# A hybrid encoder layer on one core: seven of eight chunks of the second feed-forward product in Strassen's form, with the weight sums and halves made by GpSimd

## What is computed

```python
x = layer_norm(x, ln_in_g, ln_in_b)
z = x @ w_in                                   # 1024 -> 3088 columns, three head groups
mix = concat(gla(z), stick_breaking_attention(z), short_conv(z)) @ w_out
x = layer_norm(ALPHA * x + mix, ln1_g, ln1_b)
ff = square(relu(x @ w_up)) @ w_down           # 1024 -> 4096 -> 1024
y = layer_norm(ALPHA * x + ff, ln2_g, ln2_b)
```

## Time and profile before

| what | value |
|---|---|
| median of 3 runs | 2981.42 us (2979.93 to 2982.21) |
| the profiled execution, own time | 2985.28 us |
| its span | 2983.5 us |
| TensorE busy | 2712.3 us, 91% of the span, 13798 matmuls |
| VectorE, ScalarE, GpSimd busy | 50%, 35%, 6% |
| granted TensorE clock, mean | 0.95 of full |
| DMA, mean over the span | 171 GB/s |

### The profile page before, as it was taken

One profiled execution on the slowest core, in us unless ns is written; L12 is line 12 of the kernel. 1 busy time (PEld: TensorE's weight loads), 2 busy tenths in 40 slices (PEclk: granted clock), 3 DMA queues, 4 the chain that ended last, 5 costly groups with the idle time before them and its releaser, 6 DMA issues. The chain is left out here.

```text
span 2983.5 us, 38620 instructions
## 1 busy us (share of the span) xinstructions
PE 2712.3 (91%) x13798; PEld 2251.9 (75%) x13798; DVE 1492.7 (50%) x2334; ACT 1040.6 (35%) x1812; POOL 178.5 (6%) x169
## 2 busy tenths in 40 slices
PE   6999999956773889999999999999999889999997
PEld 4787878855552678888778888777888767998985
DVE  6454443348774766656566444456444325422224
ACT  2333332323434343434324344424444321232320
POOL 1000000010000100000011000011000001000001
PEclk9999999978785899999999999999999989999998
DMA  5555454421217455756657666656665544555442
GB/s 195 177 179 169 164 171 133 138 96 37 79 48 234 152 169 183 249 184 200 217 167 236 213 212 209 206 183 204 208 227 188 170 157 155 170 171 161 163 156 95
DMA packets 357275, 509.09 MB, mean 171 GB/s; under 512 B 26656, under 2 KB 209024, under 8 KB 357088
## 3 DMA queue, kind: packets, MB, share of 16 engines
q1 hardware_dynamic: 319840, 466.74, 48.2%
q10 hardware_dynamic: 34576, 31.21, 3.1%
q0 software_dynamic: 2672, 8.66, 0.9%
HBM read 412.07 MB, written 94.45 MB: 170 GB/s over the span
## 5 line engine op out<-in xcount | busy, mean ns | idle before, releaser
L1736 DVE SCALAR_TENSOR_TENSOR p_res<-p_res,p_ps_d 128x512 f32<-128x512 f32 (+1 forms) x340 | 232.1, 685 | 470.5 <-PE p_ps_d L113 464.0
L111 PE MATMUL p_ps_u<-p_xh,p_wh 128*128 128x512 f32 (+1 forms) x1280 | 453.6, 354 | 5.3 <-DVE p_xl L1787 5.3
L112 PE MATMUL p_ps_u<-p_xh,p_wl 128*128 128x512 f32 (+1 forms) x1280 | 452.4, 353 | 0.0
L113 PE MATMUL p_ps_u<-p_xl,p_wh 128*128 128x512 f32 (+1 forms) x1280 | 451.9, 353 | 0.0
L111 PE MATMUL p_ps_d<-p_wh,p_hh 128*128 128x512 f32 (+1 forms) x1088 | 433.1, 398 | 16.6 <-DVE p_res L1736 14.6
L112 PE MATMUL p_ps_d<-p_wh,p_hl 128*128 128x512 f32 (+1 forms) x1088 | 429.4, 395 | 0.0
L113 PE MATMUL p_ps_d<-p_wl,p_hh 128*128 128x512 f32 (+1 forms) x1088 | 428.8, 394 | 0.0
L1650 ACT ACTIVATE p_wh<-p_wst 128x1024 fp32r<-128x1024 f32 x288 | 293.9, 1049 | 274.1 <-PE p_ps_d L113 225.7
L1794 DVE TENSOR_TENSOR p_r<-p_r 128x512 f32<-128x512 f32 (+1 forms) x160 | 95.8, 599 | 464.1 <-ACT p_hh L1680 464.0
L1673 ACT ACTIVATE p_r<-p_ps_u 128x512 f32<-128x512 f32 (+1 forms) x160 | 83.8, 524 | 577.4 <-PE p_ps_u L113 577.4
L111 PEld LDWEIGHTS p_ps_u<-p_xh,p_wh 128*128 128x128 f32 x1280 | 241.8, 189 | 35.6 <-DVE p_xl L1787 6.2
(11 more groups left out here) (161 smaller groups left out, 4299.4 us busy)
## 6 DMA issues: line engine op xcount, KB each, us to landing
p_wl<-wlo_scratch SPq DMA_DIRECT2D x216, 512.0 KB, 5.1
p_wst<-in_w_up SPq DMA_DIRECT2D x128, 512.0 KB, 6.0
p_wst<-in_w_down SPq DMA_DIRECT2D x128, 512.0 KB, 4.7
wlo_scratch<-p_wl SPq DMA_DIRECT2D x72, 512.0 KB, 3.6
p_wst<-in_w_in SPq DMA_DIRECT2D x128, 256.0 KB, 3.4
p_kk<-ks_scratch SPq DMA_DIRECT2D x84, 256.0 KB, 6.2
p_vv<-vs_scratch SPq DMA_DIRECT2D x84, 256.0 KB, 4.7
p_wst<-in_w_out SPq DMA_DIRECT2D x32, 512.0 KB, 5.7
```

What stands on the lines that cost most here:

```text
L111: pe.matmul(out, lhs_hi, rhs_hi, start=first, stop=False, skip_group_check=skip)
L112: pe.matmul(out, lhs_lo, rhs_hi, start=False, stop=False, skip_group_check=skip)
L113: return pe.matmul(out, lhs_hi, rhs_lo, start=False, stop=last, skip_group_check=skip)
L1736: dve.scalar_tensor_tensor(out=acc, in0=acc, scalar=scale, in1=ps_d[:c, d % DB, :], op0=ALU.mult, op1=ALU.add).then_inc(d_free, 1)
```

## The change

**The second product.** A chunk's hidden block (512 tokens by 512 hidden columns) is cut in four quarters, the weights too, and for chunks 0 to 6 seven products of sums of quarters (Winograd's variant, `PRODUCTS`) take the place of eight. A step `product` is two token tiles by two hidden tiles by 512 columns: 12 matmuls. Partial results stay in the PSUM banks and each product adds on to them, and every product's bank is added to `res` by VectorE. Chunk 7 (`PLAIN`) stays as it was, in `down` steps. The 64 tokens of the fifth tile have the plain form as well (`rest`).

**The hidden block.** ScalarE writes ReLU and its square as fp32 to `y`; a new step `split` after the fourth `up` makes four sums (VectorE) and the halves of seven blocks (ScalarE highs, VectorE lows). `mix` rows are staged in `y` too, so their loads wait for the low half of `a22` of chunk 7.

**Its weights.** The sums and both halves of all units of `w_down` are made once, in `phase_in`, by GpSimd, and stored to DRAM as pairs (1 MB for a unit, 60 units); the tail loads pairs and nothing of `w_down` is split there. GpSimd's work goes in 16 steps `halve` ("quads", half a chunk each), put into `order` at equal distances by the matmul columns. The units of `w_up` and `w_out` are split in the first group as before, and stored and loaded back as pairs as well.

**Banks and rings.** `ps_u` and `ps_d` become five banks `ps_d`; `wh` and `wl` become `wp` (four pairs); the stages are two rows of `res`. The planner prices a `product` at 2.7, a `rest` at 1.4.

```diff
+NF = 4
+NCH = D_FF // P // NF
+PLAIN = NCH - 1
+PRODUCTS = ((0, "b11", "a11"), (1, "b21", "a12"), (2, "t2", "s2"), (3, "t1", "s1"), (4, "t3", "s3"), (5, "b22", "s4"), (6, "t4", "a22"))
...
+        quads = [(c, i) for c in range(PLAIN + 1) for i in range(2)]
...
+        began = [x for x, st in enumerate(order) if st[0] == "unit"][len(by_chunk[0]) + 1]
+        spread, passed, n_quad = order[:began], 0.0, 0
...
+                while n_quad < len(quads) and passed * (len(quads) + 0.5) >= n_quad:
+                    spread.append(("halve", n_quad))
+                    n_quad += 1
...
+            def make_halves(x, n, unit, block):
+                c, i, _ = x
+                if n >= 2:
+                    pool.wait_ge(p_out[n % 2], 16 * (n // 2))
+                pool.tensor_copy(ppair[:, n % 2, 0, :], block).then_inc(p_hi, 1)
+                pool.wait_ge(p_hi, n + 1)
+                pool.tensor_tensor(ppair[:, n % 2, 1, :], block, ppair[:, n % 2, 0, :].bitcast(F32), ALU.subtract).then_inc(p_lo, 1)
+                pool.wait_ge(p_lo, n + 1)
+                pool.dma_start(wd_dram[8 * c + DOWN_UNITS.index(unit)].rearrange("p e (f n) -> p e f n", f=2)[:, :, i, :],
+                               ppair[:, n % 2, :, :].bitcast(F32)).then_inc(p_out[n % 2], 16)
...
+            def make_down_weights(x):
+                c, i, n = x
+                pool.wait_ge(p_in, 16 * (quad_no[c, i] + 1))
...
+                for k, (unit, block) in enumerate((("b11", b11), ("b12", b12), ("b21", b21), ("b22", b22))):
+                    make_halves(x, n + k, unit, block)
+                if c != PLAIN:
...
+                    pool.tensor_tensor(b22, b22, b12, ALU.subtract).then_inc(p_sum, 1)
...
+                    pool.tensor_tensor(b12, b12, b11, ALU.subtract).then_inc(p_sum, 1)
...
+                    pool.tensor_tensor(b11, b22, b11, ALU.add).then_inc(p_sum, 1)
...
+                    pool.tensor_tensor(b21, b21, b11, ALU.subtract).then_inc(p_sum, 1)
...
+                    for k, (unit, block) in enumerate((("t3", b22), ("t1", b12), ("t2", b11), ("t4", b21))):
+                        make_halves(x, n + 4 + k, unit, block)
...
+                if what == "halve":
...
+                    make_down_weights((c, i, halves_before[x]))
+                    if x + 1 < len(quads):
+                        pool.wait_ge(p_lo, halves_before[x + 1])
+                        load_down_weights(*quads[x + 1])
                 if what == "norm_a":
...
+        def down_products(g, c):
+            steps = []
+            for n, unit, _ in PRODUCTS:
+                steps.append(("product", g, c, n, weights("down", c, unit)))
+                if unit == "b22" and len(gtiles[g]) > 4:
+                    steps.append(("rest", g, c, weights("down", c, "b12")))
+            return steps
...
             for c in range(NCH - 1):
                 ffn += [up(g, c + 1, f) for f in range(2)]
-                ffn += down(g, c, 0) + down(g, c, 1)
-                if c == NCH - 2 and more:
-                    ffn += [("mix_load", g + 1, k) for k in range(4)]
-                ffn += [up(g, c + 1, f) for f in range(2, NF)]
+                ffn += down_products(g, c)
+                ffn += [up(g, c + 1, f) for f in range(2, NF)] + [("split", g, c + 1)]
             if more:
+                ffn += [("mix_load", g + 1, k) for k in range(4)]
                 ffn += out_steps(g + 1)
...
                     elif g:
-                        sp.wait_ge(d_mm, down_end[(g - 1, NCH - 2)])
+                        sp.wait_ge(blk_lo, lows_of(g - 1, PLAIN, "a22"))
...
+                    wait_unit_used(sp, u)
+                    wait_unit_stored(sp, u)
...
+                    sp.dma_start(wp[:, u % WRING, :, :].bitcast(F32), pair).then_inc(w_arrived[u % WRING], 16)
...
+                elif what == "product":
+                    g, c, n, u = at
...
+                    pe.wait_ge(blk_lo, lows_of(g, c, block))
+                    wait_halves(pe, u)
...
+                    for x in range(2):
+                        b = bank_of[(st, x)]
+                        if bank_free[(st, x)]:
+                            pe.wait_ge(*bank_free[(st, x)])
+                        for i in range(2):
+                            high, low = (t[:, place_of(block), i, P * x:P * x + P] for t in (sh, sl))
+                            mm = split_product(pe, ps_d[:, b, :], high, low, wp[:, u % WRING, 0, 512 * i:512 * i + 512], wp[:, u % WRING, 1, 512 * i:512 * i + 512],
+                                               i == 0 and n in (0, 1, 3), i == 1, skip=True)
+                        mm.then_inc(d_mm, 1)
```

More of the change, by code:

```diff
@@ L234, in phase_in @@
             order += x
+        quads = [(c, i) for c in range(PLAIN + 1) for i in range(2)]
+        quad_no = {q: x for x, q in enumerate(quads)}
+        halves_before = [0]
+        for c, i in quads:
+            halves_before.append(halves_before[-1] + (4 if c == PLAIN else 8))
+        began = [x for x, st in enumerate(order) if st[0] == "unit"][len(by_chunk[0]) + 1]
+        spread, passed, n_quad = order[:began], 0.0, 0
+        total = sum(units[st[1]]["n"] if "m0" in units[st[1]] else 512 for st in order[began:] if st[0] == "unit")
+        for st in order[began:]:
+            if st[0] == "unit":
+                while n_quad < len(quads) and passed * (len(quads) + 0.5) >= n_quad:
+                    spread.append(("halve", n_quad))
+                    n_quad += 1
+                passed += (units[st[1]]["n"] if "m0" in units[st[1]] else 512) / total
+            spread.append(st)
+        order = spread
+        assert n_quad == len(quads)
         n_a = n_d = n_conv = n_slot = n_k = 0
@@ L545, in _ @@
             pool.wait_ge(cs_out, 64)
+            for q in range(2):
+                pool.wait_ge(p_out[q], 16 * (halves_before[-1] // 2))
             for q in range(2):
@@ L1363, in phase_tail @@
             dense += ffn
-        cost = {"up": 5.4, "down": 2.7, "out": 2.7, "pause": 2.7}
+        cost = {"up": 5.4, "down": 2.7, "product": 2.7, "rest": 1.4, "out": 2.7, "pause": 2.7}
         mixed = [i for i, st in enumerate(dense) if st[0] == "mix" and st[2] == 0]
@@ L1428, in phase_tail @@
                 add_attention(group_end[st[1]])
-            if st[0] in ("up", "down", "out"):
+            if st[0] in ("up", "down", "product", "rest", "out"):
                 order.append(st)
@@ L1667, in _ @@
                     g, c, f, u = at
+                    room = hidden_room(g, c, f)
+                    if room:
+                        act.wait_ge(blk_lo, room)
+                    elif f == 0:
+                        act.wait_ge(mix_lo, KT * (g + 1))
+                    if g == 3 and c and f == 0:
+                        act.wait_ge(rest_lo, c)
                     for x, (o, cc) in enumerate(moving(GROUPS[g][1])):
```

403 lines of the change are left out of this document (280 added, 123 removed).

## The result

| | kernel before | with the change |
|---|---|---|
| median of 4 runs each | 2981.82 us | 3058.44 us (3056.66 to 3068.38) |
| ratio (of the means) | | 1.0265, 95% interval 1.0242 to 1.0288 |
| span of the profiled execution | 2983.5 us | 3054.9 us |
| TensorE matmuls | 13798 | 13462 |
| last matmul of `phase_in` ends at | 629.7 us | 764.1 us |

The change makes the kernel 2.65% slower. The two last rows split it: `phase_in` loses 134.4 us, the tail gains 61.6, and the phase between them, some 277 us in both, loses nothing. Forecast were +85 and -32.

The account below looks back on a forecast made before the run. TensorE's count of issued matmuls was taken to bound phase_in and tail. Phase_in +85, matmuls -75.7, transfers +25, next group +12, adds +8, last chunk +2, lighter load -3 gave +53: 3034 us, range 2945 to 3115.

Parts of the forecast that it names:

- third rival: GpSimd sets the length of phase_in: the stretches give 143 us and the clock 14, time 3107 us; chance 0.13.
- Matmuls: Second product in the tail: 336 fewer matmuls at 0.225 us each on a busy TensorE, -75.7 us.
- The quad: GpSimd in phase_in: copies, products, sums and stores of half a chunk take 30 us (24 to 36).
- The five stretches: Places in phase_in where quads stand between a norm's store and the next transposes, so TensorE waits: 70.6 us in all.
- A: Phase_in, units 5.1 to 10, first quad and next load: needs 36.5 us, room 23.5, +13.0.
- C: Phase_in, units 30.1 to 35, one quad with its load hidden: needs 30 us, room 23.5, +6.5.
- B: Phase_in, units 18.1 to 27, two quads and a load: needs 66.5 us, room 45, +21.5.
- D: Phase_in, units 41.6 to 52, two quads and a load: needs 66.5 us, room 53, +13.5.
- E: Phase_in, units 59.1 to 69, two quads and a load: needs 66.5 us, room 50.4, +16.1.
- The half clock: After each of five phase_in pauses TensorE runs at half clock for some 14 matmuls, 2.8 us each: 14 us.
- The weights' transfers: Tail: 1 MB pairs land every 3.19 us, slower than a product's 2.7, so runs of seven fall behind: +25 us (0 to 70).
- The way into the next group: Tail, ahead of `out`: mix rows are asked for later, +3 us and 1 more at half clock, three times: +12 (6 to 24).

Follow-up runs that it names:

- e9: The change with quads left whole, but the next load in two rows, each asked for as soon as its row is free: 3042.52 us, ratio 1.0209.
- e2: The change with the input norm's power left out, VectorE copying the variance in place of GpSimd's power; quads whole: 3030.48 us, ratio 1.0164.
- e8: e2 with one more edit: the input norm's normalised rows are stored by SyncE, not GpSimd: 2972.64 us, ratio 0.9966.
- e11: The change with pieces, third pair buffer, later transposes, earlier end and rings given back, plus a 256 KB copy behind each pair load: 2964.08 us, ratio 0.9941.
- e3: The change with GpSimd's copies, products and sums left out, its loads, stores and semaphores kept: 2944.98 us, ratio 0.9877.

## Why the prediction was right, and which terms were wrong in size

The direction and the cause were right, and 3058 lies in the range. That the sum came so near is in part luck: `phase_in`'s +134 is nearer to what the third rival made of it (143 and 14) than to the +85 of the sum, and a tail dearer on paper than on the chip made up for it. The sum of +53 was 18 too small: the profiled executions differ by 71.4 us (3056.7 less 2985.3), the medians by 76.6. By terms:

- **Matmuls.** 336 fewer, -75.7: as put.
- **The quad.** Q was to be 30 us. The 14 whole ones took 29.0 to 38.1, 33.3 on the mean. The copy was right at 0.75. The two-input product was mis-sized, 1.38 instead of 1.16 and 1.40 to 1.51 in the sums: the excess against VectorE was put at 2 us a quad, but the product and sums alone give 12 x 0.25 = 3, and the issue of a store took 0.69 instead of 0.57. The forecast had a halving bound by the landing of a store, 3.1 us each. It took 3.1, but as the engine's own 0.75 + 1.38 + 0.69 and 0.3 between them; for landings GpSimd waited 28.3 us in all quads together. That the two agree is chance. The load landed in 6.6 to 11.3, about 8, not 6.5.
- **The five stretches.** Forecast 13.0, 21.5, 6.5, 13.5 and 16.1, together 70.6; measured 19.9, 35.1, 9.3, 27.2 and 32.2, together 123.7, each at the place named. The time that GpSimd needed in each was 42.1, 76.2, 33.3, 74.3 and 73.0 us, where the prediction had 36.5, 66.5, 30, 66.5 and 66.5. That is 33 of the 53 us that were missing. Less the rooms of 23.5 and 23.5, A and C give 18.6 and 9.8, close to what was measured. The rooms of B, D and E come out 4, 6 and 10 us smaller than computed, and this is the step of the walk that was wrong: it let GpSimd begin a stretch when TensorE came to that unit. By TensorE's count of matmuls, GpSimd began its first quad of B, D and E at units 19.0, 43.5 and 60.9, not 18.1, 41.6 and 59.1 (in A and C at 5.6 and 30.3, for 5.1 and 30.1). In B and D the norm ahead was late by itself, and TensorE too waited for it:

```profile
170.44 0.76 PE L640 MATMUL p_ps_t<-p_ident,p_xn 128*128 128x128 f32 x5 [2.12 <-DVE p_xn L470]
...
361.80 0.88 PE L640 MATMUL p_ps_t<-p_ident,p_xn 128*128 128x128 f32 x6 [2.49 <-DVE p_xn L470]
```

  In E the first quad waited for its load:

```profile
487.77 0.61 POOL L563 CAST p_ppair<-p_praw 128x512 fp32r<-128x512 f32 x1 [5.12 <-DMA p_praw<-in_w_down]
```

  E also holds one of the units that aren't 24 matmuls: the 16 gate columns make one of 16, 1.8 us shorter than the 5.4 taken. What made the norms ahead of B and D late was not tested. e9, whose expectation used the same rooms, missed in the same direction.
- **The second string.** The walk through the order counted only the power. e2 and e8 show the store of the row to be worth some 35 us of waits once the power is out of the way. In the change no wait for it shows: the waits there are for the power.
- **The half clock** was put at 14. The granted clock fell to 0.67 in the window of the longest pause, but what is left of +134.4 after the seven waits at transposes (123.7 and two small ones of together 4.6) is 6.
- **The weights' transfers** were put at +25, and this is the term that was most mis-sized in the tail: it came to 9.4. The profile names a pair as what ended TensorE's wait only once; the other waits for pairs are among those that it puts down to "issue":

```profile
PE p_ps_d L121 <- issue: 44.5, 13, 12.5
...
PE p_ps_d L121 <- DMA p_wp<-wp_scratch: 0.8, 1, 0.8
```

  Of the 13, three are the pauses ahead of `out` (35.2 us) and one follows a low half of VectorE's. The other nine, 8.6 us, all end 0.09 us after a pair has landed. The longest of them, with the pair that was issued at 2180.0 and landed at 2187.24:

```profile
2187.33 0.77 PE L121 MATMUL p_ps_d<-p_wp,p_sh 128*128 128x512 f32 x1 [2.78 <-issue]
```
```profile
L1720 SPq DMA_DIRECT2D p_wp<-wd_scratch x1: 377/377/377, 2180.0 to 2180.0; - x1
...
DMA to landing us min/median/max: 7.2/7.2/7.2
```

  The price of 3.19 us for 1 MB came from a share of 0.65 at 214 GB/s, traffic that had the 512-byte pieces and small loads in it. Of the 158 gaps under 3.6 us between landings of pairs in the change, the median is 2.64 us, and a quarter are of 2.48 or less. The timeline of one run has issues at 1879.4 and 1882.2 with these times to landing; the landings are 2.46 us apart in the records, unrounded:

```profile
L1720 SPq DMA_DIRECT2D p_wp<-wp_scratch x1: 319/319/319, 1879.4 to 1879.4; - x1
...
DMA to landing us min/median/max: 6.3/6.3/6.3
```
```profile
L1720 SPq DMA_DIRECT2D p_wp<-wp_scratch x1: 319/319/319, 1882.2 to 1882.2; - x1
...
DMA to landing us min/median/max: 6.1/6.1/6.1
```

  e11 bears the working out in the main: with landings 3.15 us apart such waits are 28.9 us, and the whole costs 34 more. The Trainium skill's 425 GB/s (DMA: Bandwidth & Descriptors, Bandwidth), by which the prediction said that these 25 us would fall away, is what it has for 16 MB; for 1 MB it has 341, by which a pair would take an estimated 3.1 us. The trace bears out the higher one: 1.05 MB in 2.48 us is 423 GB/s. But the term didn't fall away whole.
- **The way into the next group** was put at +3 each, 4 with the clock. The pauses ahead of `out` went from 6.2, 5.3 and 5.2 to 12.5, 11.5 and 11.2 us, +6.2 on the mean. The loads went out at 1574.58, 7.0 us after the last matmul of `up` began, where the prediction had 4.3. One step that failed is "a low (0.7)": the loads wait for the low half that stands last, behind three others, 1.7 us after the highs. In the timeline of ScalarE, VectorE and SyncE:

```profile
1570.62 2.19 ACT L1854 ACTIVATE p_sh<-p_y 128x512 fp32r<-128x512 f32 x4
```
```profile
1571.53 3.02 DVE L1989 TENSOR_TENSOR p_sl<-p_y,p_sh 128x512 fp32r<-128x512 f32 x4
```
```profile
1574.58 7.62 SPq L1749 DMA_DIRECT2D p_y<-mixt_scratch  x6
```

  Another 1.3 us are an attention step's three activations, which stood ahead of the highs (1569.19 to 1570.6). The four rows had landed by 1580.5, 5.9 us after the first was issued (5.3 was taken).
- **Adds** were put at +8. They had the other sign: the waits of a `down` for VectorE's add, 14.6 us in ten times before, are 1.9 in one with five banks.
- The last chunk's +2 was 0.7. The -3 for the lighter load of ScalarE and VectorE was not measured by itself.

The tail's terms as measured, -75.7 + 9.4 + 18.5 - 12.7 + 0.7 = -59.8, come within 2 us of the -61.6. Waits of attention steps and the time at the lower clock changed a little too and are not in this sum.

So two errors of some size stood against each other, by luck: `phase_in` was 49 us too cheap, the tail 30 us too dear. Had the transfers been priced by the faster rate, the forecast of 3034 would have been 3009, further off.

## What to carry to other kernels

Work that is given to an idle engine must be cut so fine, and its buffers be so many, that no short instruction for others stands long behind it: with the pieces, a third buffer, later transposes and an earlier end the same arithmetic went from 134 us of loss to 6, at a load of 82% of the engine. List everything that the critical chain takes from that engine, its stores too, and give the engine's end a margin where a phase ends for all. And price a queue at full load by rows in which it carries the same kind of transfer: a mean over mixed traffic gave 3.19 us for a pair that lands 2.5 to 2.6 after the one before. Hold waits that the profile puts down to "issue" against the landings: nine of ten waits for pairs stood there.

## What was not expected of the hardware

- GpSimd's arithmetic on SBUF and VectorE's subtraction of two SBUF operands (128x512) slow each other by more than the one pair of rows showed. VectorE's went from 685 ns (at most 695, in e3) to a mean of 991 in the change, 1122 in e2 between 50 and 700 us, with single ones of 2401; GpSimd's product from 1160 to 1378. The Trainium skill (SBUF — State Buffer, Who interferes with whom) has the rule that an engine of the two that comes second waits for the whole instruction of the other; here VectorE's instruction of 2401 ns began at 686.47, 0.44 us ahead of a sum of GpSimd, and yet ended 0.56 us behind that sum, as the one in the earlier trace rows did by 0.55. So by the records the one that began first was held; one other is above 2.1 us.

```profile
L483 DVE TENSOR_TENSOR p_wl<-p_wst,p_wh x1: 2401/2401/2401, 686.5 to 686.5; 128x512 fp32r<-128x512 f32 x1
```
```profile
686.91 1.41 POOL L579 TENSOR_TENSOR p_praw<-p_praw 128x512 f32<-128x512 f32 x1
```

- The copy of 128x512 fp32 on GpSimd takes 748 ns, a bit over half of its two-input product.
- Loads of 1 MB with rows of 8 KB landed 2.48 us apart or less in a quarter of the gaps when several were under way, while one took 4.6 to 11.4 us from issue to landing, 6.1 in the median.
